# A hybrid decoder step on one core: sample attention ahead of prompt attention, and more of one key search in the feed-forward pass

## What is computed

```python
def decoder_layer(x, pe, mixer, ...):
    x = x + 0.5 * swiglu(rms_norm(x, g_ffn1), w1_gate, w1_up, w1_down)
    mixed, state = mixer(rms_norm(x, g_mix) @ w_in)
    x = x + mixed @ w_out
    x = x + 0.5 * swiglu(rms_norm(x, g_ffn2), w2_gate, w2_up, w2_down)
    gate = jax.nn.sigmoid(rms_norm(x, g_ple) @ w_ple_gate)
    return x + gate * (pe @ w_ple_proj), state
...
def indexer_select(iq, iw, ik, qpos, topk):
    logits = jnp.einsum('bthd,bld->bthl', iq, ik) * (IDX_DIM ** -0.5)
    score = jnp.einsum('bth,bthl->btl', iw * (N_IDX_HEADS ** -0.5), jax.nn.relu(logits))
    adm = jnp.arange(ik.shape[1])[None, :] <= qpos[:, None]
    _, idx = lax.top_k(jnp.where(adm[None], score, -jnp.inf), topk)
    return idx, idx <= qpos[None, :, None]
```

## Time and profile before

| | us |
|---|---|
| median of 3 runs | 3026.08 (3020.22 to 3026.2) |
| profiled execution | 3023.26 |
| its span (first to last instruction) | 3021.5 |
| PE busy in the span | 2636.0 (87%) |
| DVE, ACT, POOL busy | 1427.7, 1005.3, 1008.3 |
| granted TensorE clock, mean | 0.937 of full |

### The profile page before, as it was taken

How to read it: one execution, slowest core, us unless ns; L and a number is a source line. 1 busy time by engine, 2 the same in 40 slices (tenths; PEclk the granted TensorE clock), 3 DMA queues, 4 the chain that set the end, 5 groups by cost and what they waited for, 6 DMA issues and landing times. The chain is left out here.

```text
span 3021.5 us, 41472 instructions
## 1 busy us (share of the span) xinstructions
PE 2636.0 (87%) x15166; PEld 2285.3 (76%) x15166; DVE 1427.7 (47%) x3227; ACT 1005.3 (33%) x1581; POOL 1008.3 (33%) x521
## 2 busy tenths in 40 slices
PE   4999998787887878888898966888999999999997
PEld 4999998566666666666786656777889988778887
DVE  3233324679774212222366787776333343442354
ACT  4222224422333233332345312333444233332242
POOL 4333333223223333333344222122122344454341
PEclk9999998898898889998998978998999999999999
DMA  4333234221111333433142111111111323223222
GB/s 144 96 103 97 92 102 133 100 78 56 63 50 49 104 111 102 124 119 100 61 143 72 63 51 49 43 49 43 43 55 58 105 77 98 90 93 105 91 70 74
DMA packets 157038, 253.40 MB, mean 84 GB/s; under 512 B 15010, under 2 KB 101283, under 8 KB 156835
## 3 DMA queue, kind: packets, MB, share of 16 engines
q1 hardware_dynamic: 154144, 247.02, 25.4%
q10 hardware_dynamic: 2690, 3.72, 0.3%
HBM read 240.34 MB, written 18.73 MB: 86 GB/s over the span
## 5 line engine op out<-in xcount | busy, mean ns | idle before, releaser
L728 POOL TENSOR_TENSOR w_lo<-raw,w_hi 128x1024 fp32r<-128x1024 f32 x250 | 603.3, 2415 | 1075.9 <-ACT w_hi L828 1075.4
L1421 PE MATMUL ps<-xna_hi,w_hi 128*128 128x288 f32 x2000 | 614.2, 307 | 38.1 <-DVE tb L1133 14.1
L1422 PE MATMUL ps<-xna_lo,w_hi 128*128 128x288 f32 x2000 | 602.2, 301 | 0.0
L1423 PE MATMUL ps<-xna_hi,w_lo 128*128 128x288 f32 x2000 | 601.7, 301 | 0.0
L1421 PEld LDWEIGHTS ps<-xna_hi,w_hi 128*128 128x128 f32 x2000 | 389.5, 195 | 52.9 <-DVE tb L1133 14.7
L1421 PE MATMUL ps<-xnb_hi,w_hi 128*128 128x512 f32 x1000 | 420.1, 420 | 10.8 <-DVE tb L1133 5.7
L1422 PE MATMUL ps<-xnb_lo,w_hi 128*128 128x512 f32 x1000 | 403.9, 404 | 0.0
L1423 PE MATMUL ps<-xnb_hi,w_lo 128*128 128x512 f32 x1000 | 402.8, 403 | 0.0
L728 POOL TENSOR_TENSOR d_lo<-raw,d_hi 128x1024 fp32r<-128x1024 f32 x90 | 216.5, 2426 | 532.5 <-ACT d_hi L828 532.5
L1422 PEld LDWEIGHTS ps<-xna_lo,w_hi 128*128 128x128 f32 x2000 | 389.0, 194 | 0.2
L1423 PEld LDWEIGHTS ps<-xna_hi,w_lo 128*128 128x128 f32 x2000 | 388.0, 194 | 0.0
(11 more groups left out here) (288 smaller groups left out, 4236.6 us busy)
## 6 DMA issues: line engine op xcount, KB each, us to landing
raw<-in_w_gu SPq DMA_DIRECT2D x176, 512.0 KB, 3.5
raw<-in_w_d SPq DMA_DIRECT2D x88, 512.0 KB, 3.5
raw<-in_w_ring SPq DMA_DIRECT2D x74, 512.0 KB, 3.5
pages<-in_vk_pages SPq DMA_DIRECT2D x256, 128.0 KB, 2.6
idx_flat<-in_idx_pages SPq DMA_DIRECT2D x256, 32.0 KB, 2.1
idxp<-idx_flat SPq DMA_DIRECT2D x8, 1024.0 KB, 8.1
x_spill<-xa SPq DMA_DIRECT2D x1, 2304.0 KB, 8.9
xa<-x_spill SPq DMA_DIRECT2D x4, 576.0 KB, 6.2
```

Of the source, the lines that this page charges most:

```text
L728: g_.tensor_tensor(lo[slot][:, :, :], raw[l % 2][:, :, :], hi[slot][:, :, :].bitcast(f32), ALU.subtract).then_inc(lo_done, 1)
L1421: mm(out, shi, mhi, start=first, stop=False)
L1422: mm(out, shi, mlo, start=False, stop=False)
L1423: return mm(out, slo, mhi, start=False, stop=last)
```

## The change

Order. In the first pass for group 1 the rest of the sample search (bits 12 to 31, ties, queries) comes first, then the samples' attention with one bit of search A behind every second group, then the attention of blocks 0 to 3. Search A leaves the first input projection, which takes sample bits 0 to 11 instead of 0 to 7. `EARLY` goes from 20 to 8: 24 instead of 12 bits of B1 stand in the second pass. `norm` gets an empty group between `sums` and `spread`; the sample index's head matrix `wm` moves behind the index products. `ks` goes to the front of its group, the shares of a sample pair (`vw`, `vf`) two or three groups ahead of `vo`, and a block's queries four heads ahead of the block.

Steps. The sum of squares stays in PSUM bank 5 in 11 of 15 cases. A rotation works in its PSUM bank, and the bank is free when the rotation is done. A unit's diagonal `dg` is written by ACT, not DVE. A search bit does its two-column steps column by column and drops one, a sample bit merges two. `K_RING` is 3 instead of 4, and some tiles move.

```diff
-K_RING, V_RING = 4, 8
+K_RING, V_RING = 3, 8
-EARLY = 20
+EARLY = 8
@@ norm
-        groups = [[("sums", k, c)], [("spread", k, c)] + ...
+        groups = [[("sums", k, c)], [], [("spread", k, c)] + ...
@@ prompt
-            if now and now[1] == 0:
-                groups.append([("qb", now[0])])
+            if s == 0:
+                groups += [[("qb", now[0])], [], []]
+            elif now and now[1] == 4 and now[0] + 1 in blocks:
+                groups.append([("qb", now[0] + 1)])
@@ samples
-                    put(s, (4, ("ks", *divmod(4 * ch + i + 1, 4))))
+                    put(s, (-1, ("ks", *divmod(4 * ch + i + 1, 4))))
...
+                put(end + 2, (5, ("vw", ch // 4)))
+                put(end + 3, (5, ("vf", ch // 4)))
@@ order, input projection of group 0
-            side.append(g + [("bt", "A", j) for j in range(3 * kc, 3 * kc + 3)])
+            side.append(g)
-        side += [[("st", j)] for j in range(8)]
+        side += [[("st", j)] for j in range(12)]
@@ order, first pass for group 1
+        search = [[("st", j)] for j in range(12, 32)] + [[("sties", i)] for i in range(3)] + [[("qs",)]]
+        groups = self.samples()
+        for j in range(32):
+            groups[6 + 2 * j].append(("bt", "A", j))
         units = self.prompt(BLOCKS[0])
+        units[3].append(("room", "A"))
+        units[4].append(("bties", 2))
+        units[6].append(("bties", 3))
-        first = weave(first, self.samples() + [[], [("mix", 0)], [("back", 0)]], 68, -8)
-        ev += weave(first, early, 2, 66)
+        first = weave(first, groups + units + [[], [("mix", 0)], [("back", 0)]], 51, -3)
+        ev += weave(first, search, 2, 50)
@@ ACT, square
-                    A(ssq[g][:, own(c)], x[g][:, m, own(c)], ACT.Square).then_inc(sq_done, 1)
+                    A(ps[:, 5, 0:CH[c][1]] if in_psum(k, c) else ssq[g][:, own(c)], x[g][:, m, own(c)], ACT.Square).then_inc(sq_done, 1)
@@ ACT, transposed
+                if i == 0:
+                    u = n("pv", b, r)
+                    act.wait_ge(ri_done, u)
+                    wait(act, pv_done, u - 2)
+                    A(dg[:, r % 2, :], ident[:, 0, :], ACT.Copy, scale=ri[:, r % 2:r % 2 + 1]).then_inc(dg_done, 1)
@@ DVE, rotate
-                    v.tensor_tensor(zt[:, own(c)], z, cos, ALU.mult).then_inc(in_dve, 1)
+                    v.tensor_tensor(z, z, cos, ALU.mult)
-                    v.tensor_tensor(dst, zt[:, own(c)], zs[:, own(c)], ALU.add).then_inc(rope_done, 1)
+                    v.tensor_tensor(dst, z, zs[:, own(c)], ALU.add).then_inc(rope_done, 1)
@@ DVE, threshold_bit
-                if j < 31:
-                    v.tensor_scalar(with_bit[:, :], cand[:, :], 1 << (30 - j), None, ALU.bitwise_xor)
-                dve.drain()
-                v.tensor_scalar(drop[:, :], reached[:, :], TOPK - 0.5, 1.0 if j else -1.0, ALU.is_lt, ALU.mult)
                 dve.drain()
                 for i in range(2):
+                    v.tensor_scalar(drop[:, i:i + 1], reached[:, i:i + 1], TOPK - 0.5, float(2 ** (31 - j)) if j else -1.0, ALU.is_lt, ALU.mult)
@@ PE
+                    if key[0] < T_V and key[0] != T_IK:
+                        pe.wait_ge(rope_done, n("rope", key[0], c))
@@ SP, kv_load
                     sp.wait_ge(smask_ready, 1)
-                    sp.wait_ge(pv_done, n("pv", 3, 7))
```

More of the change, by code:

```diff
@@ L173, in norm @@
     def norm(self, k, c, apart=False):
-        groups = [[("sums", k, c)], [("spread", k, c)] + [("scale", k, c, m) for m in range(4)], [("scale", k, c, m) for m in range(4, KT)]]
+        groups = [[("sums", k, c)], [], [("spread", k, c)] + [("scale", k, c, m) for m in range(4)], [("scale", k, c, m) for m in range(4, KT)]]
         return groups if apart else [e for g in groups for e in g]
@@ L424, in program @@
         s_w, s_f = small[:, 28:32], small[:, 32:36]
-        cand, with_bit, drop = [small_i[:, 2 * j:2 * j + 2] for j in range(3)]
+        cand, drop = [small_i[:, 2 * j:2 * j + 2] for j in range(2)]
         s_cand, s_with_bit, s_drop = [small_i[:, 6 + j:7 + j] for j in range(3)]
@@ L578, in x_final, with in_psum @@
                 eng.wait_ge(ple_done, n("pj", m, c))
+        def in_psum(k, c):
+            return (k, c) not in ((1, 2), (2, 1), (4, 0), (4, 1))
         def diag_of(k, c):
@@ L836, in square @@
                         wait(act, sums_done, n("sums", k - 1, c))
-                    A(ssq[g][:, own(c)], x[g][:, m, own(c)], ACT.Square).then_inc(sq_done, 1)
+                    if in_psum(k, c):
+                        wait(act, ssq_done, added_up[0])
+                        added_up[0] = n("ssq", k, c, KT - 1)
+                    A(ps[:, 5, 0:CH[c][1]] if in_psum(k, c) else ssq[g][:, own(c)], x[g][:, m, own(c)], ACT.Square).then_inc(sq_done, 1)
                     return
@@ L1012, in _ @@
                     "sil": sample_logits, "siw": sample_scores, "vtr": values, "qb": queries, "qk": logits, "ptr": transposed,
-                    "ks": keys, "smax": weights, "vt": sample_transposed, "vo": shares, "mix": mix, "pe": embed}
+                    "ks": keys, "smax": weights, "vt": sample_transposed, "vw": shares, "mix": mix, "pe": embed}
             for e in events:
@@ L1234, in threshold_bit @@
                 count(hits if name != "B1" else early_hits if j < EARLY else late_hits, blocks, cand[:, :].bitcast(f32), ALU.is_ge)
-                if j < 31:
-                    v.tensor_scalar(with_bit[:, :], cand[:, :], 1 << (30 - j), None, ALU.bitwise_xor)
-                dve.drain()
-                v.tensor_scalar(drop[:, :], reached[:, :], TOPK - 0.5, 1.0 if j else -1.0, ALU.is_lt, ALU.mult)
                 dve.drain()
                 for i in range(2):
-                    v.tensor_scalar(cand[:, i:i + 1], drop[:, i:i + 1], 31 - j if j else 0, (with_bit if j < 31 else cand)[:, i:i + 1],
-                                    ALU.logical_shift_left, ALU.bitwise_xor)
+                    v.tensor_scalar(drop[:, i:i + 1], reached[:, i:i + 1], TOPK - 0.5, float(2 ** (31 - j)) if j else -1.0, ALU.is_lt, ALU.mult)
+                dve.drain()
+                for i in range(2):
+                    v.tensor_scalar(cand[:, i:i + 1], drop[:, i:i + 1], 1 << (30 - j) if j < 31 else 0, cand[:, i:i + 1], ALU.bitwise_xor, ALU.bitwise_xor)
                 dve.drain()
@@ L1343, in inverse @@
                 dve.wait_ge(exp_done, u)
+                wait(dve, dg_done, u - 2)
                 v.reciprocal(ri[:, s:s + 1], rs[:, s:s + 1]).then_inc(ri_done, 1)
[L1345 to L1347 removed]
             def attended(b, r):
```

64 lines of the change are left out of this document (32 added, 32 removed).

## The result

| | before | after |
|---|---|---|
| median, us | 3026.14 (3020.22 to 3027.29, 4 runs) | 2927.94 (2922.61 to 2934.7, 4 runs) |
| profiled execution / span | 3023.26 / 3021.5 | 2924.44 / 2922.7 |
| PE / DVE busy | 2636.0 / 1427.7 | 2615.3 / 1313.0 |
| granted clock, mean | 0.937 | 0.943 |

The ratio is 0.968, with a 95% interval of 0.9654 to 0.9707: 98 us gained where 161 were forecast. The time lies inside the range of 2790 to 2960, 63 us above the forecast and 8 us from rival (1): it is in the band from 2905 to 2960, which had a chance of 0.18, and not in the forecast's own from 2830 to 2905, which had 0.56.

What follows compares the result with a forecast made beforehand. PE carries the span, with SP taking over in the sample part and DVE bounding the search part. -29 - 85 - 12 - 20 - 13 - 3 = -162 from 3023.3 gives 2861, or 2865 us as a median; range 2790 to 2960.

Steps and rivals of the forecast that it cites:

- rival (1): Sample part: the wait for POOL becomes one for loads, only a third gained; 400 us, 2920 in all; chance 0.18.
- the first pass for group 1: Search part, sample part and rest together: 151 + 345 + 198 = 694 us against 779, -85.
- sign of being wrong: Either a sample part above 400 us, or a second pass longer than 643 us.
- Rest of the pass: First pass for group 1 after the samples: remaining products, last sample groups and 32 prompt units, 198 us.
- second input projection: 1576:1751: twelve bits of blocks 4 and 5 move out, diagonals come later behind their sums; -12 us.
- Sample part: First to last sample logits, 1029:1453: SP takes over as the bound; 345 us, between 278 and 398.
- all of the 75.5 us [...] gone: Sample part: PE's waits for POOL's low part vanish; with other waits and clock gains, 398 would become 278 us.
- SP's terms: Sample part: 64 pieces x 2.75, 16 number fetches x 5.2 and 24 weight loads x 0.6 = 274 us.
- Search part: From 730 to the first sample logits: DVE is the bound at 139 us, plus about 12; 151 us.
- First input projection: 494:730: 32 bits leave, four sample bits come, the head matrix moves; -29 us, between -12 and -40.
- Second pass: 1751:2394: 128 us to block 4's first logits, DVE's small steps and diagonals cheaper; -20, between -45 and +15.
- Norms: Additions of squares in PSUM save DVE about 45 us, mostly hidden; third pass -13, between -3 and -15.

Runs made afterwards that it cites:

- p1: Kernel after the change, with the next 16 page numbers fetched behind a fourth piece's loads, not ahead of the next ones; 2922.7 us.
- p2: Kernel after the change, with no page numbers fetched: samples read fixed pages, four issues a piece as before; 2905.8 us.
- p3: Kernel after the change, with fixed pages, no number fetches and two 256 KB issues per piece instead of four; 2903.4 us.
- x1: p3 with PE multiplying the keys' high part twice, so it never waits for POOL's difference, which is still computed; 2840.7 us.
- c3: p1 with PE doing the four high-part matmuls of a piece before it waits for POOL's difference; nothing left out; 2911.9 us.
- c5: c3 with page numbers fetched four at a time behind each piece's loads, the first four ahead of the wait for the masks; 2892.5 us.
- u2: Kernel after the change with EARLY back at 20, so 12 bits of blocks 4 and 5 return to the second input projection; 2928.3 us.
- b1_ks_first: Kernel before the change with only the K copy moved to the front of its group, old stage order and ring of 4 kept; 3018.9 us.
- u1_ks_last: Kernel after the change with the copy of the next keys put back behind the weights' transposes; 2943.8 us.
- d1: p1 with the 64 key differences on DVE, behind its read of the logits before, instead of on POOL; 2920.8 us.

## Why the prediction was right, and where not

The direction and the range held; the size did not (98 us for 161), and the time is in the range only because the range had room for rival (1), whose mechanism is a part of what happened; the other part, POOL's splits, no rival had named, so that it landed there is in part luck. Nearly all of the miss is one term, the first pass for group 1: -29 for -85. Of the signs that the prediction named for being right, two held: ACT now waits for pages, and no addition of squares through PSUM takes more than 0.70 us. Four did not: PE's wait for the low part (64.3 us, not below 20), the time per sample piece (383 / 64 = 6.0 us, not 5 to 5.7), the first sample logits (871, not near 850), and the third pass's waits for its two diagonals (one of 3.6 us, none over 2 forecast). Neither sign of being wrong appeared. By its steps:

- **Rest of the pass, second input projection**: 198 and 200, -12 and -12. The products hide the 2.1 us bits of search A in the sample part, where PE waits for DVE's read of the logits 0.2 us in all, and the ties cost nothing that shows.
- **Sample part, 345 against 383.** The failed step is "all of the 75.5 us [...] gone", with SP as the one thing that takes over. SP did take part (rival 1's mechanism): without the numbers 16 us of this stretch go (p1 to p2). But the chain was counted as one queue. Once K_hi is early, the low part comes from POOL, which is in a split of 2.4 us just when it is wanted, and PE still waits 44.7 us for it here. In p3, with half the issues and no numbers, it is still 40.6, and only 0.4 of that is for late pages. The prediction also counted on nearly all of the clock's tenth (35 us); 0.85 instead of 0.90 was granted. The 4.7 us per piece in its sum for 345 stands on no row, and a mean of 0.90 between full and half clock is a fifth of the time at the lower level, not a tenth. x1 shows where the step was right in principle: without PE's wait for POOL, and with the quicker loads, the sample part is 311 us at a clock of 0.96. None of the rivals had loads and POOL late side by side.
- **SP's terms.** 2.75 us per piece was right as a time and wrong as a price: half the issues gave 2 us. 5.2 us per fetch of numbers was the part that mattered: without them the sample part is 16 us shorter (p1 to p2), and 10 come from the fetches in fours alone (c3 to c5).
- **Search part, 151 against 167.** DVE's work to the masks was sized well: 146 us (703.2 to 848.8) for 139. "The first loads and the queries, about 12" is mis-sized, at 22: PE waits 19.6 us in one wait ahead of the first sample logits. It is not for the masks, which are there 2.6 us before PE stops, but for SP, whose queue has weight loads ahead of the pages; the last of them waits for POOL's splits and goes out at 858. Then come the 16 numbers (5.3 us), four transfers, copy and difference. Leaving the numbers out or fetching them earlier took 4 to 5 us of it (p2, c5).
- **First input projection, -22 against -29.** The wait for the head matrix (9.8 us) is gone. PE's waits for the convolutions are 7.8 us and were 3.9, where 8 more were forecast; in all PE idles for 22.6 us instead of 42.1. What is missing is the clock, which rose to 0.91 only, from 0.89.
- **Second pass, -28 against -20.** The moved bits cost what they gain elsewhere (u2), as 128 us for the start (130 measured) said. The mis-sized term is the small steps: "32 x 0.3" took the mean of the kernel before. At the start of the second pass a two-column step costs 656 ns where the mean had 389, and undoing steps and diagonals costs 39 us, not 18. Of the 98 us gained it is the largest single piece that these runs found; the copy's place (16 us) and the sums (14) come next. The new order of the first pass, the rotation in PSUM and the ring of 3 were not undone, so their share is not shown. The diagonal's copy on ACT takes 0.40 us, 25 us in all, where 20 was taken and 0.29 us estimated.
- **Norms.** DVE gains 47 us (119.7 to 72.3), 45 predicted. The third pass has -7 for -13: its two waits for a diagonal take 5.0 us together, the longest 3.6, where 9.9 was before and nothing over 2 us was forecast. The end has 9.0 us of such waits in 3 instead of 3.4 in one, and is 3 us longer, where 3 less were forecast for the rest. The empty group was not tried alone, so the reason is open.

The rows for the search part (SP's issues) and for the third pass (PE's waits):

```profile
844.44 13.85 SPq L610 DMA_DIRECT2D raw<-in_w_gu  x3
863.61 10.03 SPq L692 DMA_DIRECT2D pages<-in_vk_pages  x12
```

```profile
PE ps L1549 <- DVE diag L1069: 5.0, 2, 3.6
```

## What to carry to other kernels

Where a chain of four engines feeds a product, taking one late link away shows only the next: split each wait by what every engine of the chain was doing, bound each link by an experiment that drops the wait for it, and count on the gain only when all that are late go. Before you move an instruction to another engine, check in the trace that what held it up does not hold it there too. Spread rare long work on an in-order queue (16 numbers at once) into short pieces before you shorten it. Price two-element steps on DVE by the stretch they stand in, not by the kernel's mean, and write them one column at a time where POOL is busy; where POOL is idle, two at once are cheaper.

## What was not expected of the hardware

- Less idle time did not bring a higher granted clock where the pauses became fewer and longer. In b1_ks_first 47 waits for the low part became 20, PE idled for 16 us less (61 of 422 for 77 of 424), and 0.90 became 0.84. From u1_ks_last to the kernel after, 46 waits became 16, PE idled for 17 us less, and 0.87 became 0.85. Between p3 and x1, 52 us shorter with the same matmuls, 0.87 became 0.96 and PE's busy time fell from 316 to 289 us.
- Four DMA issues of 128 KB or two of 256 KB per piece make no difference (2905.8 and 2903.4 us).
- A two-column integer step on DVE took 162 to 172 ns alone and up to 2.4 us when it met one of POOL's splits, and then ended with it; one-column steps took 149 and 209 ns either way.
- The difference of two tiles in SBUF, moved to DVE (d1), took 0.69 us alone and up to 2.46 beside a split of POOL: leaving POOL's queue did not take it out of POOL's way.
